# First and fourth norm from column sums, spread by diagonal products, with a new order of the opening

## The reference, cut to what matters

```python
def rmsnorm(x, g):
    xf = x.astype(jnp.float32)
    y = xf * lax.rsqrt(jnp.mean(xf * xf, axis=-1, keepdims=True) + EPS)
    return (y * g.astype(jnp.float32)).astype(x.dtype)

xn = rmsnorm(h, norm1_g[l]) * (1 + sc1) + sh1
h = h + g1 * token_mix(xn @ w_in[l], k_c, v_c, lp, cos, sin)
h = h + g2 * sq_relu_mlp(rmsnorm(h, norm2_g[l]) * (1 + sc2) + sh2, w_ff1[l], w_ff2[l])
```

## Time and profile before

| what | us |
|---|---|
| median of 3 runs | 1350.1 |
| the profiled execution | 1349.34 |
| its span | 1347.5 |
| TensorE busy in the span | 1318.7 |
| VectorE busy | 884.2 |
| ScalarE busy | 551.4 |
| GpSimd busy | 208.6 |

### The profile page before, as it was taken

One profiled execution on the slowest core, in us unless ns is written; L12 is line 12 of the kernel. 1 busy time (PEld: TensorE's weight loads), 2 busy tenths in 40 slices (PEclk: granted clock), 3 DMA queues, 4 the chain that ended last, 5 costly groups with the idle time before them and its releaser, 6 DMA issues.

```text
span 1347.5 us, 19330 instructions
## 1 busy us (share of the span) xinstructions
PE 1318.7 (98%) x7858; PEld 1099.0 (82%) x7858; DVE 884.2 (66%) x1212; ACT 551.4 (41%) x855; POOL 208.6 (15%) x177
## 2 busy tenths in 40 slices
PE   7999999999999999999999999999999999999998
PEld 3567767888778888888888888888679999899998
DVE  5575677877548666645675556378866888675663
ACT  6652563332233323532113331144555444563553
POOL 1161000904100152000000003300005404100012
PEclk8999999999999999999999999999999999999999
DMA  9343204555442352324554457324235647466562
GB/s 374 131 137 117 94 1 160 161 183 176 158 139 63 125 169 82 110 94 138 204 176 154 134 186 258 110 83 156 83 110 183 226 134 280 138 190 203 189 202 80
DMA packets 55432, 205.26 MB, mean 152 GB/s; under 512 B 6277, under 2 KB 6661, under 8 KB 53808
## 3 DMA queue, kind: packets, MB, share of 16 engines
q1 hardware_dynamic: 52848, 193.70, 43.2%
q0 software_dynamic: 2208, 9.81, 2.0%
q10 hardware_dynamic: 288, 0.52, 0.1%
HBM read 200.86 MB, written 3.15 MB: 151 GB/s over the span
## 4 chain that ended last, share of the span: by engine, by line
PE 92%; DVE 3%; ACT 2%; DMA 1%; issue 1%; POOL 0%; SPq 0%; DVEq 0%; ACTq 0%
PE ps L1664 27%; PE ps L1666 27%; PE ps L1665 26%; PE ps L2015 3%; PE ps L2043 1%; PE ps L2026 1%; DMA pairs<-in_pairs 1%; DVE wl L1107 1%; PE ps L2147 1%; PE ps L2135 1%; PE ps L1693 1%; PE ps L1857 1%; PE ps L1733 1%; DVE k_t L1384 0%; PE ps L1706 0%
## 5 line engine op out<-in xcount | busy, mean ns | idle before, releaser
L1664 PE MATMUL ps<-xh,wh 128*128 128x256 f32 (+2 forms) x1416 | 475.8, 336 | 4.3 <-DVE xl L1195 2.4
L1665 PE MATMUL ps<-xl,wh 128*128 128x256 f32 (+2 forms) x1416 | 469.1, 331 | 0.0
L1666 PE MATMUL ps<-xh,wl 128*128 128x256 f32 (+2 forms) x1416 | 469.0, 331 | 0.0
L1107 DVE TENSOR_TENSOR wl<-raw,wh 128x1024 fp32r<-128x1024 f32 (+2 forms) x272 | 355.4, 1310 | 122.6 <-ACT wh L759 120.0
L759 ACT ACTIVATE wh<-raw 128x1024 fp32r<-128x1024 f32 (+2 forms) x272 | 283.5, 1044 | 296.2 <-PE ps L1666 296.2
L1664 PEld LDWEIGHTS ps<-xh,wh 128*128 128x128 f32 (+1 forms) x1416 | 265.9, 188 | 40.7 <-issue 13.2
L1666 PEld LDWEIGHTS ps<-xh,wl 128*128 128x128 f32 (+1 forms) x1416 | 265.7, 188 | 28.1
L1665 PEld LDWEIGHTS ps<-xl,wh 128*128 128x128 f32 (+1 forms) x1416 | 265.7, 188 | 27.4 <-issue 1.2
L1664 PE MATMUL ps<-hid_h,wh 128*128 128x512 f32 (+1 forms) x512 | 170.9, 334 | 0.0
L1665 PE MATMUL ps<-hid_l,wh 128*128 128x512 f32 (+1 forms) x512 | 170.3, 333 | 0.0
L1666 PE MATMUL ps<-hid_h,wl 128*128 128x512 f32 (+1 forms) x512 | 170.3, 333 | 0.0
(11 more groups left out here) (270 smaller groups left out, 1535.5 us busy)
## 6 DMA issues: line engine op xcount, KB each, us to landing
raw<-in_units SPq DMA_DIRECT2D x262, 512.0 KB, 4.2
mod_ring<-in_mod_units SPq DMA_DIRECT2D x62, 512.0 KB, 3.9
pairs<-in_pairs SPq DMA_DIRECT2D x6, 1024.0 KB, 14.4
gap_hy<-in_mod_units SPq DMA_DIRECT2D x12, 512.0 KB, 5.0
raw<-in_units SPq DMA_DIRECT2D x6, 384.0 KB, 3.1
h<-in_x SPq DMA_DIRECT2D x4, 512.0 KB, 8.1
mod_ring<-in_pairs SPq DMA_DIRECT2D x2, 1024.0 KB, 15.5
counts<-in_counts POOLq DMA_DIRECT2D x2, 1024.0 KB, 5.1
```

The source lines that it names most:

```text
L1107: dve.tensor_tensor(wl[:, g % SLOTS, 0:n], raw[:, g % SLOTS, 0:n], wh[:, g % SLOTS, 0:n].bitcast(F), ALU.subtract)\
L1664: pe.matmul(dst, w_h, m_h, start=first, stop=False)
L1665: pe.matmul(dst, w_h, m_l, start=False, stop=False)
L1666: return pe.matmul(dst, w_l, m_h, start=False, stop=last)
```

## The change

The sums of v = 0 and v = 3 become columns (`column_sums`), one token per partition. The root and the reciprocal then run over 4 or 2 elements. VectorE multiplies the identity by each reciprocal column (`diagonal`), and TensorE multiplies ones by these diagonals (`spread_rstd`), which puts the reciprocals of all tokens on every partition in bank 6. The products read them there. For v = 0, VectorE later copies them to `rstd`. For v = 3 the spread stands behind three of the eight conditioning units. An unneeded root is put ahead of the waits of v = 1 and v = 3, and behind the first sigmoid. In the opening, three warm products become two and stand behind pair 0, the first units are multiplied in smaller pieces between pairs 1 to 3, ScalarE and VectorE follow this order, and the load of `f_w3` waits for pair 1.

```diff
@@ gpsimd @@
             pool.wait_ge(h_in_s[3], 16)
-            pool.dma_start(f_w3[:, :], f_w3_in).then_inc(f_w3_in_s, 16)
             pool.dma_start(decay[:, :], decay_in[0:1, :].broadcast_to([128, 2 * HY])).then_inc(decay_in_s[0], 16)
             pool.wait_ge(pair_loaded[1], 16)
+            pool.dma_start(f_w3[:, :], f_w3_in).then_inc(f_w3_in_s, 16)
@@ scalar: std, root and the opening @@
+                    if v % 2:
+                        act.activation(small[:, 0:1], eps[:, 0:1], ACT.Sqrt)
                     act.wait_ge(squares_added, added_before(v + 1))
...
+                if v in BY_COLUMNS:
+                    nb = NORM_T[v] // 128
+                    sums = ps[:, SUM_BANKS[v]:SUM_BANKS[v] + nb, 0]
+                    act.activation(rstd[:, 0:nb], sums, ACT.Sqrt, bias=eps[:, 0:1], scale=1.0 / D).then_inc(std_ready, 1)
+                    return
...
-            act.activation(small[:, 0:1], params[:, 0:1], ACT.Copy).then_inc(act_bank_free, 2)
+            act.activation(small[:, 0:1], eps[:, 0:1], ACT.Sqrt).then_inc(act_bank_free, 2)
...
-            for g in range(2):
-                split(g)
+            split(0)
+            norm_full(0, 0)
+            norm_hi(0, 0)
+            split(1)
             filter_sines(0)
-            for m in range(KB):
-                norm_full(0, m)
-                norm_hi(0, m)
-                if m == 0:
-                    for g in range(2, WAVE):
-                        split(g)
+            copy_pair(1)
+            split(2)
+            norm_full(0, 1)
+            norm_hi(0, 1)
+            split(3)
+            for m in range(1, KB):
+                if m > 1:
+                    norm_full(0, m)
+                    norm_hi(0, m)
                 if m + 1 < KB:
                     copy_pair(m + 1)
@@ vector: norm_rstd, the products, the opening @@
+                if v in BY_COLUMNS:
+                    nb = NORM_T[v] // 128
+                    chained(dve.reciprocal(rstd[:, 0:nb], rstd[:, 0:nb]))
+                    for tb in range(nb):
+                        dve.tensor_scalar(diagonal[:, tb * 128:(tb + 1) * 128], ident, rstd[:, tb:tb + 1], None, ALU.mult).then_inc(rstd_ready, 1)
+                    dve.wait_ge(sumsq_ready, sums_before(v) + 2)
+                    return
...
+                by = ps[:, SUMSQ_BANKS[0], 0:n] if m < 2 else rstd[:, 0:n]
...
+                        by = ps[:, SUMSQ_BANKS[0], t] if v in BY_COLUMNS else rstd[:, t]
...
             norm_lo(0, 0)
-            for g in range(1, WAVE):
-                split(g)
-            for m in range(KB):
-                if m:
+            split(1)
+            chained(dve.tensor_copy(rstd, ps[:, SUMSQ_BANKS[0], :]))
+            add_pair(1)
+            split(2)
+            norm_by_rstd(0, 2)
+            norm_lo(0, 1)
+            split(3)
+            for m in range(1, KB):
+                if m > 1:
                     norm_lo(0, m)
@@ tensor @@
+            def column_sums(v, squares, first, last):
+                for tb in range(NORM_T[v] // 128):
+                    mm = pe.matmul(ps[:, SUM_BANKS[v] + tb, 0:1], squares[:, tb * 128:(tb + 1) * 128], ones[:, 0:1], start=first, stop=last)
+                return mm
+
+            def spread_rstd(v):
+                for tb in range(NORM_T[v] // 128):
+                    pe.wait_ge(rstd_ready, rstd_before(v) + tb + 1)
+                    mm = pe.matmul(ps[:, SUMSQ_BANKS[0], tb * 128:(tb + 1) * 128], ones, diagonal[:, tb * 128:(tb + 1) * 128],
+                                   start=True, stop=True)
+                mm.then_inc(sumsq_ready, 1)
...
-                mm = pe.matmul(ps[:, SUMSQ_BANKS[0], :], ones, normed[:, 2 * c, :], start=c == 0, stop=c == 3)
+                mm = column_sums(0, normed[:, 2 * c, :], c == 0, c == 3)
             mm.then_inc(sumsq_ready, 1)
+            spread_rstd(0)
             pe.wait_ge(silu_ready, 1)
             pair(0)
             turn_pair(0)
+            warm(2)
+            first = [(g, WAVE_BANKS[g]) for g in range(WAVE)]
+            wave_step(0, 0, first[:2], T, (x_split, 0))
             pair(1)
-            warm(3)
+            turn_pair(1)
+            wave_step(0, 0, first[2:3], T, (x_split, 0))
             pe.wait_ge(f_sin, 1)
             pe.matmul(ps[:, 7, 0:SEQ], f_w12[:, 1, :], f_hid[:, :], start=True, stop=True).then_inc(f_pre, 1)
-            first = [(g, WAVE_BANKS[g]) for g in range(WAVE)]
-            for m in range(KB):
+            wave_step(0, 1, first[:2], T, (x_split, 0))
+            pair(2)
+            wave_step(0, 0, first[3:], T, (x_split, 0))
+            turn_pair(2)
+            wave_step(0, 1, first[2:], T, (x_split, 0))
+            pair(3)
+            for m in range(2, KB):
...
-                mod_events(PHASES[layer, "w_out"], KB)
+                if layer:
+                    for _, i in PHASES[layer, "w_out"].tail[:SPREAD_AFTER]:
+                        mod_unit(i)
+                    spread_rstd(3)
+                    for _, i in PHASES[layer, "w_out"].tail[SPREAD_AFTER:]:
+                        mod_unit(i)
+                else:
+                    mod_events(PHASES[layer, "w_out"], KB)
```

More of the change, by code:

```diff
@@ L272, in backbone @@
         sq = norm_room[:, T:3 * T].rearrange("p (a t) -> p a t", t=T)
+        diagonal = sq[:, 0, :]
         params = alloc(ctx, "params", (PARAMS,))
@@ L560, in backbone, with sums_before, rstd_before @@
         SUMSQ_BANKS = (6, 7)
+        SPREAD_AFTER = 3
+        SUM_BANKS = {0: 0, 3: 6}
+        BY_COLUMNS = (0, 2 * DEPTH - 1)
+        def sums_before(v):
+            return parts_before(v) + sum(u < v for u in BY_COLUMNS)
+        def rstd_before(v):
+            return parts_before(v) + sum(NORM_T[u] // 128 - 1 for u in BY_COLUMNS if u < v)
         def squared_before(v):
@@ L786, in std @@
                     final_gain(KB - 1)
-                act.wait_ge(sumsq_ready, parts_before(v) + 1)
                 if v == 2 * DEPTH:
+                    act.wait_ge(sumsq_ready, sums_before(v) + 1)
                     for tb in range(SEQ // 128):
@@ L795, in root @@
                 t = NORM_PARTS[v][part]
-                act.wait_ge(sumsq_ready, parts_before(v) + part + 1)
+                act.wait_ge(sumsq_ready, sums_before(v) + part + 1)
+                if v in BY_COLUMNS:
[3 more added lines that the diff above has]
+                    return
                 act.activation(rstd[:, t], ps[:, SUMSQ_BANKS[part], 0:t.stop - t.start], ACT.Sqrt, bias=eps[:, 0:1], scale=1.0 / D)\
@@ L1081, in _ @@
                 (norm if layer == 0 else std)(2 * layer + 2)
-            act.wait_ge(rstd_ready, parts_before(2 * DEPTH) + 1)
+            act.wait_ge(rstd_ready, rstd_before(2 * DEPTH) + 1)
             act.wait_ge(gain_turned, 1)
@@ L1165, in norm_rstd @@
                 dve.wait_ge(std_ready, count)
+                if v in BY_COLUMNS:
[5 more added lines that the diff above has]
+                    return
                 dve.reciprocal(rstd[:, t], rstd[:, t]).then_inc(rstd_ready, 1)
-                dve.wait_ge(rstd_ready, count)
+                dve.wait_ge(rstd_ready, rstd_before(v) + part + 1)
             def norm_by_rstd(v, m):
                 n = NORM_T[v]
-                dve.tensor_tensor(normed[:, m, 0:n], h[:, m, 0:n], rstd[:, 0:n], ALU.mult).then_inc(normed_dve, 1)
+                by = ps[:, SUMSQ_BANKS[0], 0:n] if m < 2 else rstd[:, 0:n]
+                dve.tensor_tensor(normed[:, m, 0:n], h[:, m, 0:n], by, ALU.mult).then_inc(normed_dve, 1)
             def norm_lo(v, m):
@@ L1187, in product @@
                         t = slice(s * SEQ, (s + 1) * SEQ)
-                        last = dve.scalar_tensor_tensor(normed[:, m, t], h[:, m, t], scales[:, v, m, s:s + 1], rstd[:, t], ALU.mult, ALU.mult)
+                        by = ps[:, SUMSQ_BANKS[0], t] if v in BY_COLUMNS else rstd[:, t]
+                        last = dve.scalar_tensor_tensor(normed[:, m, t], h[:, m, t], scales[:, v, m, s:s + 1], by, ALU.mult, ALU.mult)
                     last.then_inc(normed_dve, 1)
@@ L1216, in final_norm @@
                 dve.reciprocal(rstd[:, 0:2], rstd[:, 0:2]).then_inc(rstd_ready, 1)
-                dve.wait_ge(rstd_ready, count + 1)
+                dve.wait_ge(rstd_ready, rstd_before(2 * DEPTH) + 1)
                 dve.wait_ge(gain_turned, 1)
@@ L1780, in dve_bank @@
                 return 2 + (p.dve0 + i) % 2
+            def column_sums(v, squares, first, last):
[8 more added lines that the diff above has]
+                mm.then_inc(sumsq_ready, 1)
             def rms(v, part=0):
                 t = NORM_PARTS[v][part]
+                if v in BY_COLUMNS:
+                    pe.wait_ge(squares_added, added_before(v + 1))
+                    column_sums(v, sq_sum, True, False)
+                    pe.wait_ge(h_squared, squared_before(v + 1))
+                    column_sums(v, sq[:, 0, :], False, False)
+                    pe.wait_ge(last_squared, parts_before(v) + part)
```

(2 more changed lines are left out.)

## The result

The changed kernel takes 1359.9 us (median of 5 runs, 1355.7 to 1361.8) beside 1350.1 before, a ratio of 1.0055 [1.0033, 1.0077]: **slower, and above the 1352.6 to which the range went**. The profiled execution spans 1360.0 us, 12.5 more than before.

What follows compares the result with a forecast made beforehand. The chain that ended last is 92% TensorE, so a norm is worth only TensorE's waiting. 3.2 (v = 3) + 0.46 (v = 1) - 2.2 (opening) = 1.4 us less, a median of 1348.7; range 1345.5 to 1352.6.

Steps and rivals of the forecast that it cites:

- the range: Whole kernel: median between 1345.5 and 1352.6 us, leaving out some 0.15 of the chances.
- the bound of 0.46: v = 1: the gain is only TensorE's wait, 0 to 0.46 us, as its own work holds it until 528.35.
- the sum: The prediction's added-up step times: at v = 3 TensorE starts 1.6 us earlier; at v = 1 it is held until 528.35.
- the third rival: Roots: another table is in place when the root is due, so the load stays in front; 1351.4 us, chance 0.1.
- The walk: Opening, followed step by step: first unit at 23.0, pair 2 at 31.9, step 2 at 40.3 instead of 38.06; loses 2.2 us.
- four waits of together 2.9 us: Opening, TensorE before step 2: these waits lose what it gains at 23, so it is done at 36.7 in both kernels.
- the rival with a chance of 0.15: Opening: column products bring the half level from 16 to 30, pair 2 at 36.8, loss 6.1 us; 1352.5 us, chance 0.15.
- the signs named: Right if: no load at three roots, product 0 near 18, first unit 23, pair 2's copy 33, step 2 40, v = 3 unwaited.
- the sign of being wrong that came: Opening: a half level of the clock reaching into the steps from 23 on, named as showing the forecast wrong.

Runs made afterwards that it cites:

- columns_128: The changed kernel with the column sums of v = 0 multiplying 128 columns of ones instead of one; 1353.9 us, ratio 1.002.
- columns_128_filled: columns_128 with three and six warm products filling TensorE's waits in front of unit 2 and of step 2; 1350.9 us, ratio 1.0003.
- again: The changed kernel run once more, nothing edited; 1359.4 us over 12 runs, ratio 1.0049.
- order_only_wide_sums: The changed kernel with the old wide sums, root and reciprocal for v = 0, keeping the new order and early table; 1354.9 us, ratio 1.0028.
- one_wait: The kernel before, with only ScalarE's separate wait for the sums ahead of the root taken away for v = 0 to 3; 1348.6 us, ratio 0.9987.
- envelope_back: pairs_ahead with the first envelope one block earlier, behind the copy of pair 2; 1346.0 us, ratio 0.9957.
- pairs_ahead: columns_128 with pair 1 ahead of the first unit, pair 2 ahead of units 2 and 3, and the first envelope one block later; 1347.5 us, ratio 0.9976.

## Why the prediction was wrong

**v = 3 and v = 1: right in kind.** Forecast 3.2 and 0.46, measured 2.8 to 2.9 and 0.7. At v = 3 the first product came 1.3 us earlier and not 1.6, and the clock gave 1.5 to 1.6. At v = 1 the bound of 0.46 was too low: the sum let TensorE be held until 528.35, the end that the row gives for the last sums, but in the changed kernel the first product starts at 535.82, 0.25 behind the start of those sums (535.57) and before their end in the row (536.16):

```profile
535.57 0.59 PE L1848 MATMUL ps<-norm_room,consts 128*128 128x256 f32 x2
...
535.82 0.47 PE L1702 MATMUL ps<-xh,wh 128*128 128x256 f32 x1
```

Diagonals were 0.24 each (0.22 taken), and from the end of the sums to VectorE's first product it took 2.1 us (1164.96 to 1167.07; the sum had 1.95). PSUM as an operand cost nothing (0.87 for two products, 0.88 before). No load stands in front of any of the three roots, which settles the third rival. The price of the single edits was not seen: I gave all of v = 1 to the early root, and 0.5 of the 0.7 came from the removed wait.

**The opening: the order was right, the clock wrong.** The walk said that pair 2 goes behind a full step, and that the envelope behind its copy carries the delay on. Both stand in the rows above, and at full clock its steps are met. What failed is the term that the sum left out. I wrote that TensorE "loses in four waits of together 2.9 us" what it gains at 23, and costed those waits, and the one in front of step 2 (36.7 to 40.3 in the walk), at their length alone. The lengths were right: 0.44, 0.50 and 1.74 ahead of step 2's, together 2.7, and 3.13 in front of step 2. The forecast put the half level at nothing. My own rows showed at v = 3 that a wait of 1.95 us is followed by the half level for 3.3 us, and I used that to credit v = 3 with 1.6 us, but not to charge the opening.

Laid beside columns_128 and columns_128_filled, the 7.9 us of the changed kernel come to this. At full clock the order loses 3.0 (the walk: 2.2). The first half level costs 2.0 up to the first unit. The second costs 1.3, since from there to step 2 it takes 18.98 us, and 17.64 in columns_128_filled. The third costs 1.6, since from step 2 to step 3 it takes 5.97 and took 4.42 before. In again the three cost 2.2, 2.0 and 2.5, which makes its 9.6. The later two don't need the first: columns_128 has them without it, and the waits are no longer in the changed kernel (1.74 and 3.13) than there (1.75 and 3.15).

**The thin products.** This was the rival with a chance of 0.15: half level from 16, loss 6.1. Its first part came true (15.1 to 25.3), and columns_128 shows its cause. But it ended the half level at 30 for good and saw no second and third. So the loss of 7.9 to 9.6 lies beyond the rival's 6.1. At an equal pace the kernel is 4.4 to 5.9 us slower by the traces, where I had 1.4 faster. The median rose by 7.3 (again, beside 1352.1 for the kernel before at the same time); what that is more, the two paces can make of a median.

The Trainium skill (TensorE: Matmul & The Clock Gate, What's actually happening), which says that the half rate is the default and that activity releases it, pointed at both causes. The trace agrees in kind (a granted clock of 0.50 behind the thin products and behind the waits of 1.74 and 3.13 us), though the 3.13 us of order_only_wide_sums left it at 1.00. I gave the clock a chance of 0.15 in an opening with new waits, and the rows at v = 3 spoke for more. Another rule of the Trainium skill (ScalarE: Activation LUTs, What ACT_TABLE_LOAD costs: a drain of 1.38 us on top of the load) is not seen: in one_wait the root starts at 1157.76, where the load that began at 1156.47 ends.

**The range** held the walk's own errors and one half level. Three of them, with 4.9 to 6.7 us together, were outside it. Of the signs named, the roots without a load and the start behind v = 3 held. Product 0 (19.01), the first unit (25.39), the copy of pair 2 (37.10) and step 2 (44.37) came later than named, and the half level that reaches into the steps from 23 on was the sign of being wrong that came.

## What to carry to other kernels

An early start on the bounding engine is worth something only if it has work until the old start; if it meets new waits instead, price each wait of about 1.7 us or more with a half clock that may follow (1.3 to 2.5 us each here), and fill it with products nobody reads where it can't be removed. A product that sums into one column can stream 128 at the same time, and here it kept the clock. When an operation gets short, look for what was hidden under it, and before a computation is rewritten, try whether a doubled wait or a table load placed elsewhere gives the same.

## What the runs showed of the hardware

- With products of one column the granted clock fell in a stretch that shows PE busy throughout (15 to 16 in the changed kernel, clock 0.56). With the same passes at 128 columns it stayed at 1.00. In the other four kernels with thin sums it fell at 14.8 to 16.8 us, in two of them 0.3 and 1.0 us behind the last thin product.
- A wait of 2.01 us (envelope_back), 1.74 and 3.13 (changed), 1.95 brought the half level; one of 1.14 (one_wait) did not. In pairs_ahead one of 1.68 did not either, and in order_only_wide_sums not even one of 3.13, so the length of a wait alone doesn't tell.
- A table load runs ahead of the wait that its activation carries: it started at 1156.47 in one_wait, 0.7 us before the sums it is for were there.
- The products of 256 columns have two spacings, 113.3 and 117.8 ns, at full clock in both, and an execution keeps one of them through the last stretch. What draws it stays open; no run was made for it.
